# A hybrid decoder trunk on one core: start-up transfers put in line, the first statistics moved into the third weight tile, attention scores of four heads issued together, and the squares before the pool mixer summed on VectorE

## What is computed

```python
def rmsnorm(x, g):
    return x * rsqrt(mean(x * x, -1) + EPS) * g
def swiglu(h, w_gate, w_up, w_down):
    return (silu(h @ w_gate) * (h @ w_up)) @ w_down
for i in range(2):
    x = x + 0.5 * swiglu(rmsnorm(x, g[i, 0]), ...)
    h = rmsnorm(x, g[i, 1])
    x = x + (moba_attention(h, w_qkv, w_o) if i == 0 else pool_mixer(h, pool_w, pool_scale))
    x = x + 0.5 * swiglu(rmsnorm(x, g[i, 2]), ...)
return rmsnorm(x, final_gain)
```

## Time and profile before

| | |
|---|---|
| median of 3 executions | 890.85 us (889.71 to 890.87) |
| profiled execution, its time | 889.62 us |
| its span, first to last instruction | 887.7 us |
| TensorE busy | 874.7 us (99%) |
| VectorE, ScalarE busy | 630.9 us (71%), 468.8 us (53%) |
| mean granted TensorE clock | 0.995 of full speed |

### The profile page before, as it was taken

How to read it: one execution, slowest core, us unless ns; L and a number is a source line. 1 busy time by engine, 2 the same in 40 slices (tenths; PEclk the granted TensorE clock), 3 DMA queues, 4 the chain that set the end, 5 groups by cost and what they waited for, 6 DMA issues and landing times.

```text
span 887.7 us, 12466 instructions
## 1 busy us (share of the span) xinstructions
PE 874.7 (99%) x5252; PEld 768.7 (87%) x5252; DVE 630.9 (71%) x718; ACT 468.8 (53%) x557; POOL 34.1 (4%) x49
## 2 busy tenths in 40 slices
PE   7999999999999999999999999999999999999997
PEld 6888888889998988888888888888889988888885
DVE  5997776668777598777667697776666698777452
ACT  5765554445555566555544475555544675555441
POOL 1580000000000000000000000000000000000000
PEclk9999999999999999999999999999999999999999
DMA  7786656555544438665565566565566177565431
GB/s 247 228 244 196 190 178 197 181 190 175 159 142 143 143 97 256 188 190 190 168 205 181 176 204 193 188 190 188 177 200 191 49 217 222 188 218 187 154 119 47
DMA packets 154167, 159.69 MB, mean 180 GB/s; under 512 B 2888, under 2 KB 152448, under 8 KB 154112
## 3 DMA queue, kind: packets, MB, share of 16 engines
q1 hardware_dynamic: 152672, 157.30, 55.8%
q10 hardware_dynamic: 1440, 1.60, 0.5%
HBM read 157.84 MB, written 1.05 MB: 179 GB/s over the span
## 4 chain that ended last, share of the span: by engine, by line
PE 97%; DVE 1%; ACT 0%; issue 0%; POOL 0%; DVEq 0%; POOLq 0%
PE psum L413 95%; PE psum L694 1%; PE psum L680 1%; PE psum L587 0%; DVE w_lo L1151 0%; DVE x L1157 0%; PE psum L580 0%; DVE soft L979 0%; PE psum L453 0%; ACT xg L777 0%; DVE w_lo L1143 0%; ACT scratch L848 0%; DVE band L1080 0%; DVE h_all L1232 0%; DVE scratch L1083 0%
## 5 line engine op out<-in xcount | busy, mean ns | idle before, releaser
L413 PE MATMUL psum<-xg,w_hi 128*128 128x512 f32 (+1 forms) x1664 | 491.4, 380 | 2.9 <-DVE w_lo L1143 2.9
L960 DVE TENSOR_TENSOR w_lo<-raw,w_hi 128x2048 fp32r<-128x2048 f32 (+1 forms) x150 | 336.3, 2243 | 119.8 <-ACT w_hi L768 119.8
L413 PEld LDWEIGHTS psum<-xg,w_lo 128*128 128x128 f32 x1536 | 289.6, 189 | 62.7
L768 ACT ACTIVATE w_hi<-raw 128x2048 fp32r<-128x2048 f32 (+1 forms) x150 | 279.5, 1865 | 92.0 <-PE psum L413 92.0
L413 PE MATMUL psum<-xg,w_lo 128*128 128x256 f32 x1536 | 313.3, 279 | 0.0
L413 PEld LDWEIGHTS psum<-xg,w_hi 128*128 128x128 f32 x1664 | 254.8, 189 | 5.8 <-issue 4.7
L413 PE MATMUL psum<-h_all,w_hi 128*128 128x512 f32 (+1 forms) x656 | 189.4, 374 | 0.7 <-DVE h_all L1232 0.7
L413 PEld LDWEIGHTS psum<-h_all,w_lo 128*128 128x128 f32 x592 | 111.4, 188 | 23.4
L413 PE MATMUL psum<-h_all,w_lo 128*128 128x256 f32 x592 | 121.8, 278 | 0.0
L413 PEld LDWEIGHTS psum<-h_all,w_hi 128*128 128x128 f32 x656 | 100.3, 189 | 1.5 <-issue 1.5
L803 ACT ACTIVATE scratch<-psum 128x512 f32<-128x512 f32 x44 | 26.2, 595 | 86.0 <-PE psum L413 86.0
(11 more groups left out here) (108 smaller groups left out, 489.8 us busy)
## 6 DMA issues: line engine op xcount, KB each, us to landing
raw<-in_ffn_w_up_dram SPq DMA_DIRECT2D x43, 1024.0 KB, 5.3
raw<-in_ffn_w_gate_dram SPq DMA_DIRECT2D x42, 1024.0 KB, 5.3
raw<-in_ffn_w_down_dram SPq DMA_DIRECT2D x24, 1024.0 KB, 5.1
raw<-in_attn_w_qkv_dram SPq DMA_DIRECT2D x12, 1024.0 KB, 5.1
raw<-in_ffn_w_down_dram SPq DMA_DIRECT2D x20, 512.0 KB, 4.3
raw<-in_ffn_w_down_dram SPq DMA_DIRECT2D x12, 768.0 KB, 4.3
raw<-in_attn_w_o_dram SPq DMA_DIRECT2D x4, 1024.0 KB, 5.0
band<-in_x_dram SPq DMA_DIRECT2D x4, 256.0 KB, 5.4
```

The lines of the kernel that those rows point to most:

```text
L413: return nc.tensor.matmul(out, stationary, moving, start=start, stop=stop, skip_group_check=True)
L768: nc.scalar.activation(w_hi[:, n % SPL, 0:size], raw[:, n % RAW, 0:size], ACT.Copy).then_inc(hi_split, 1)
L960: nc.vector.tensor_tensor(w_lo[:, n % SPL, 0:size], raw[:, n % RAW, 0:size], w_hi[:, n % SPL, 0:size].bitcast(f32), ALU.subtract).then_inc ...
```

## The change

In the head, SyncE waits until the second piece of tile 0 has landed before it issues tiles 1 and 2. TensorE does 8 + 3 + 5 idle transposes around the gains and the first two pieces of x in place of 12 ahead of them, and transposes pieces 2 and 3 of x ahead of k = 0 and k = 2 (ahead of k = 2 and k = 4 before). The first statistics move behind the first half of tile 2 (gate of group 1), tile 3 follows, and VectorE splits tile 3 before it takes the mean.

In the first three quads of attention all four heads' scores are issued together, then the q and k products, then the four heads' transposes, the v product, and the four heads' values; `prob` and `probT` get four buffers. ScalarE does all four heads' exponentials before it rounds weights, VectorE all four heads' softmax before it splits them.

At the pool boundary the squares are summed on VectorE (the last two chunks one by one), and TensorE needs two products with ones, in the middle of the last pool product. Half of `pool_u` is scaled by VectorE. The up tile of the last FFN is no longer split in the FFN before, but by halves inside `mixer_boundary`. ScalarE loads the root's table at the start of `down`. FFNs 1 to 3 start when their gate tile is split, not gate and up tile both.

```diff
+            sp.wait_ge(piece_loaded[1], 16)
             ffn(0, 0, 0)
...
-                            if norm == 0 and k % 2 == 0 and 0 < k < DC - 2:
-                                x_transposes(k // 2 + 1)
+                            if norm == 0 and k % 2 == 0 and k < DC - 4:
+                                x_transposes(k // 2 + 2)
...
                 if f == 0:
                     column_chunks(0, 0, range(DC))
                     column_chunks(0, 1, range(DC))
+                    pe.wait_ge(x_done, DC // 2)
+                    column_chunks(1, 0, range(DC // 2))
+                    pe.wait_ge(x_done, DC)
                     statistics(norm)
...
-                else:
-                    weights(n0 + 1)
+                    column_chunks(1, 0, range(DC // 2, DC))
+                    weights(n0 + 3)
+                    pe.wait_ge(newton, 1)
+                    column_chunks(1, 1, range(DC))
+                else:
+                    weights(n0)
...
-            for _ in range(12):
-                nc.tensor.transpose(psum[:, 2, 0:P], ident[:, :], ident[:, :])
-            x_transposes(0)
+            idle_transposes(8)
...
+            x_transposes(0)
+            idle_transposes(3)
             x_transposes(1)
+            idle_transposes(5)
...
                 scores(j, 0)
-                between(0)
-                transposes(j, 0)
-                scores(j, 1)
-                between(1)
-                values(j, 0)
-                transposes(j, 1)
                 if j < QUADS - 1:
+                    scores(j, 1)
+                    between(0)
+                    between(1)
+                    transposes(j, 0)
+                    transposes(j, 1)
                     between(2)
+                    values(j, 0)
                     values(j, 1)
...
+                        if g == NPG - 1 and t == 0 and m == 1:
+                            statistics(4)
...
-                if g == 1:
-                    for c in range(DB):
-                        token_squares(4, c)
...
+            def load_root():
+                nc.scalar.activation(table[:, 1:2], table[:, 0:1], ACT.Sqrt)
+
             def down(f):
+                load_root()
...
-                for t in range(TT):
-                    last = nc.scalar.activation(pool_u[:, g, t, :], psum[:, g, t * GW:(t + 1) * GW], ACT.Copy,
-                                                scale=rstd_p[:, t:t + 1])
-                last.then_inc(pool_u_scaled, 1)
+                nc.scalar.activation(pool_u[:, g, 0, :], pool_acc(g, 0), ACT.Copy,
+                                     scale=rstd_p[:, 0:1]).then_inc(pool_u_scaled[0], 1)
...
+                nc.vector.tensor_scalar(pool_u[:, g, 1, :], pool_acc(g, 1), rstd_p[:, 1:2], None,
+                                        ALU.mult).then_inc(pool_u_scaled[1], 1)
...
-            def mixer_boundary(norm, scalar, per_chunk=False):
+            def split_lo_ahead(n, half):
+                dve.wait_ge(hi_split, n + 1)
+                part = slice(half * ROWS // 2, (half + 1) * ROWS // 2)
+                nc.vector.tensor_tensor(w_lo[:, n % SPL, part], raw[:, n % RAW, part], w_hi[:, n % SPL, part].bitcast(f32),
+                                        ALU.subtract).then_inc(lo_split if half else up_half, 1)
+
+            def mixer_boundary(norm, scalar, per_chunk=False, split_ahead=None):
                 for c in range(DB + 1):
+                    if split_ahead is not None and c == DB - 1:
+                        rest_chunk(norm, 2 * c - 2)
+                        rest_chunk(norm, 2 * c - 1)
+                        split_lo_ahead(split_ahead, 0)
...
             split_lo_half(2, 1)
+            split_lo(3)
             dve.wait_ge(late_T, 1)
...
-            split_lo(3)
             refine_rstd(0)
```

More of the change, by code:

```diff
@@ L442, in statistics @@
                 pe.wait_ge(sq_sum_done, FOLDS.index(norm) + 1)
-                last = mm(psum[:, b, 0:SEQ], ones[:, :], sq_sum[:, :], start=True, stop=True)
-                for t in range(TT if norm == 1 else 0):
+                if norm != 4:
+                    last = mm(psum[:, b, 0:SEQ], ones[:, :], sq_sum[:, :], start=True, stop=True)
+                for t in range(TT if norm in (1, 4) else 0):
                     last = mm(psum[:, b, SEQ + t:SEQ + t + 1], sq_sum[:, t * P:(t + 1) * P], ones[:, 0:1],
@@ L549, in ffn @@
                     column_chunks(0, 1, range(EARLY, DC))
-                for j in range(1, GROUPS):
+                for j in range(1 if f else 2, GROUPS):
                     gate_up(j)
@@ L584, in _, with idle_transposes @@
             pe.wait_ge(consts_built, 2)
-            for _ in range(12):
-                nc.tensor.transpose(psum[:, 2, 0:P], ident[:, :], ident[:, :])
-            x_transposes(0)
+            def idle_transposes(count):
+                for _ in range(count):
+                    nc.tensor.transpose(psum[:, 2, 0:P], ident[:, :], ident[:, :])
+            idle_transposes(8)
             pe.wait_ge(gains_loaded, 16)
@@ L913, in _ @@
             for j in range(QUADS):
-                for half in range(2):
-                    heads = (2 * half, 2 * half + 1)
-                    for hh in heads:
+                if j < QUADS - 1:
+                    for hh in range(QH):
                         exps(QH * j + hh)
-                    split_hi(ATT0 + 3 * j + 2 + half + SPL)
-                    for hh in heads:
+                    split_hi(ATT0 + 3 * j + 2 + SPL)
+                    split_hi(ATT0 + 3 * j + 3 + SPL)
+                    for hh in range(QH):
                         copy_probT(j, hh)
+                else:
+                    for half in range(2):
+                        heads = (2 * half, 2 * half + 1)
+                        for hh in heads:
+                            exps(QH * j + hh)
+                        split_hi(ATT0 + 3 * j + 2 + half + SPL)
+                        for hh in heads:
+                            copy_probT(j, hh)
                 split_hi(ATT0 + 3 * j + 4 + SPL)
@@ L1057, in down @@
                         add_squares(norm, pair - 1)
-                    split_lo(n + 1 + SPL)
+                    if f == 2 and pair == DB - 1:
+                        dve.wait_ge(sq_added, FOLDS.index(4) * (DB - 1) + DB - 2)
+                        nc.vector.tensor_tensor(sq_sum[:, :], sq[:, 0, :], sq[:, 1, :], ALU.add).then_inc(sq_added, 1)
+                    else:
+                        split_lo(n + 1 + SPL)
                     for d in (2 * pair, 2 * pair + 1):
@@ L1216, in _ @@
             for j in range(QUADS):
-                for half in range(2):
-                    heads = (2 * half, 2 * half + 1)
-                    for hh in heads:
+                if j < QUADS - 1:
+                    bias_and_max(j, 0)
+                    for hh in range(1, QH):
                         bias_and_max(j, hh)
-                    for hh in heads:
-                        normalise(QH * j + hh)
-                    if j == 0 and half == 0:
+                        normalise(QH * j + hh - 1)
+                    normalise(QH * j + QH - 1)
+                    if j == 0:
                         qkv_scale(0, 2)
-                    split_lo(ATT0 + 3 * j + 2 + half + SPL)
-                    if j < QUADS - 1:
-                        qkv_scale(j + 1, half)
+                    for s in range(2):
+                        split_lo(ATT0 + 3 * j + 2 + s + SPL)
+                        qkv_scale(j + 1, s)
+                else:
+                    for half in range(2):
+                        heads = (2 * half, 2 * half + 1)
+                        for hh in heads:
+                            bias_and_max(j, hh)
+                        for hh in heads:
+                            normalise(QH * j + hh)
+                        split_lo(ATT0 + 3 * j + 2 + half + SPL)
                 split_lo(ATT0 + 3 * j + 4 + SPL)
```

98 lines of the change are left out of this document (65 added, 33 removed).

## The result

The changed kernel takes 881.7 us (median of 4 executions, 881.35 to 882.02), the kernel before, on the same chip, 890.86 us (4 executions, 889.71 to 891.12). The ratio is 0.9903 with a 95% interval of 0.9891 to 0.9915: 9.2 us less. 881.2 was forecast. The profiled executions went from 889.62 to 881.35 us, 8.3 us less; the new one has a span of 879.3 us, and its mean granted clock is 0.999.

What follows compares the result with a forecast made beforehand. TensorE, busy 99% of the span, bounds the kernel. Head 4.0, attention 1.5 and pool boundary 3.5 sum to 9.0 us, taking the profiled 889.62 to 880.6 and the median to 881.2; range 878.5 to 884.5 us.

Steps and rivals of the forecast that it cites:

- The head: Start of the kernel: TensorE's start on tile 4 moves from 36.5 to 32.5 us, 4.0 us; bounds 2.3 and 4.9.
- TensorE waits 1.0 us for tile 4: Head: TensorE there at 31.7 us, VectorE's split of tile 4 done at 32.5, so a new wait of 0.8 us.
- VectorE's chain to have only one change: Head: same operations in another order, except that VectorE now waits 0.5 us for ScalarE's root.
- The rival: Head gives little, chance 0.14: late first x piece, clock fall or late halves of tile 1; 2.0 us gained, 883.2.
- Attention: First three quads: six merged blocks of scores and values save 0.25 us each, 1.5 us; bounds nothing and 3.0.
- the regroupings are neutral: Attention rival, chance 0.08: the 0.2 us is a pipeline's end, not the switch; merged blocks cost the same, 882.7.
- fall of the clock: Attention rival, chance 0.03: half-array values and scores in succession lower the clock; 6 us falls cost 9.0 us, giving 891.7.
- The pool boundary: Before the last FFN: 3.9 us less at its start, 0.4 lost behind, 3.5 us; bounds 2.0 and 4.2.
- The new wait: Pool boundary: TensorE waits for the scaled pieces behind the statistics, +0.7 us.
- The 0.4 us: Last FFN: waits from VectorE's half splits and what queues behind them, last x pair, last rests and sums, +0.4 us.
- The 1.5 us of clock: Pool boundary: the 24 matmuls behind the products with ones run at full clock, -1.5 us.
- The median: Whole kernel: the new median may lie 0 to 1.2 us over the new profile of 880.6; predicted 881.2.

Runs made afterwards that it cites:

- hold_first_fill: The changed kernel with SyncE waiting for the first gate piece in place of the second, and 8 idle transposes in place of 5: 880.97 us.
- scores_apart: The changed kernel with the second pair's scores put back behind the q product in the first three quads: 882.64 us.
- trans_apart: The changed kernel with the first pair's transposes put between the q and the k product; scores and values stay merged: 881.39 us.
- narrow_extra: The changed kernel with 14 unused products with one column of ones (28 rows) behind the second pool product: 886.08 us, a fourth execution of 3063.89 left out.
- wide_extra: The changed kernel with 30 unused idle transposes, 128 columns wide, behind the second pool product: 884.54 us.
- head_only: The kernel before with only the head's part of the change: 885.28 us, ratio 0.9952.
- attn_only: The kernel before with only attention's part of the change: 889.29 us over 12 executions, ratio 0.9984.
- pool_only: The kernel before with the pool boundary's part, the up tile's halves, the root's table and the gate-tile start of FFNs 1 to 3: 886.6 us.

## Why the prediction was right

The bottleneck was read rightly: time came from TensorE alone, and only in the three stretches named. The sum was 9.0 us, made of 4.0, 1.5 and 3.5; the profiled pair gives 3.25, 2.1 and 3.2, which is 8.55 of stage gains against 8.3 us between the two times. All three sizes were off: the head by -0.75, attention by +0.6, the boundary by -0.3. That the head's miss and attention's nearly cancel is luck.

- **The head**, 4.0 forecast, 3.25 measured. Its mechanism holds: VectorE's last piece moved by 3.55 us (forecast 3.7), the root is exposed for 0.48 us (0.5), the clock stays up, and without the idle transposes it does not. TensorE waits 1.0 us for tile 4 (0.8), but the two agree only since both engines are late: TensorE is there at 32.4 us in place of 31.7, and tile 4 can start at 33.4 in place of 32.5. The mis-sized term is the one that took VectorE's chain to have only one change: the held-back halves of tile 1 are late and cost 0.63 us. The rival named this, halves there at 10.9 to 12.3 us where VectorE wants them at 12.4; the first came at 12.2, but ScalarE's rounding of 1.06 us lies between landing and VectorE. hold_first_fill takes that wait away, and tile 4 moves by 0.4 us. The other 0.1 us is what smaller terms leave, such as the last piece, 0.15 us later than forecast.
- **Attention**, 1.5 forecast, 2.1 measured. Scores count and transposes don't, as forecast (scores_apart, trans_apart); for values only the rest of the 0.7 us speaks. The price for a merged block was 0.25 us from two rows and is 0.35 (0.7 us a quad, two blocks) or 0.38 (scores_apart). That the regroupings are neutral is out; no fall of the clock was seen behind values and scores (granted clock 1.00 from 200 to 300 us).
- **The pool boundary**, 3.9 forecast and 3.6 measured at the start of the last FFN, then 0.4 lost: 3.2. The new wait was taken at 0.7 us and costs 1.0 from start to start (0.8 in the list of waits). The 0.4 us are the size that was forecast, but the last rests and the sums, to which they were put down among others, come in time: it is two weight splits that TensorE waits for. The 1.5 us of clock in it are real for the pair of profiles, and narrow_extra against wide_extra gives 1.4. But they are not due in every execution: head_only's profile had none to lose, attn_only's lost 3 us. What the structure alone saves is 12.87 - 10.78 = 2.1 us.
- **The median**. The new profile was the fastest of its four, as was the old, so the median lies 0.35 us over it; it was taken 0.6 over, which takes back 0.25 of the 0.75 us by which the profile itself was missed.

What stays open: whether an ordinary execution is faster without the hold, what decides whether the clock falls behind the 32 narrow rows, and how the head's gain divides among the parts that weren't taken apart.

## What to carry to other kernels

Where TensorE waits for first transfers, give it cheap full-width transposes instead of idling: eight of them were worth 1.0 us here. Queue only as much behind the first needed pieces as leaves them on time, and count the engines between landing and use when a transfer is held back. Sum squares on an engine with room rather than by one-column products, and put all work on part of the array in one block. Value a part of a change by its own stage in the trace: in these profiles what the clock did elsewhere added 1.5 us to the head's 3.25 and took 2.6 us from attention's 2.1.

## What the runs showed that I had not expected

The same 32 one-column rows were followed by full clock (head_only) and by 1.2 GHz for some 3 us (before); in attn_only the clock was down for 6 to 7 us from within the rows on. The code at that place is the same. The changed kernel, without these rows, spreads by 0.7 us (881.35 to 882.02), attn_only by 4.6; but the rows aren't the only thing that makes executions differ, since pool_only has none either and spreads by 1.4.

The record of the clock can miss a fall. In attn_only's window at 10 to 12 us above it says 1.00, with 9 matmuls in 2.0 us, as many as in the window of before at 0.50; in the changed kernel there are 13. This is TensorE's timeline in that window:

```profile
9.80 1.05 PE L414 MATMUL psum<-xg,w_hi 128*128 128x512 f32 x2
10.65 0.63 PE L414 MATMUL psum<-xg,w_lo 128*128 128x256 f32 x2
```

A pair of 512 wide matmuls takes 1.05 us in place of 0.63 to 0.70, as a pair does at 9.26 us in the kernel before, where the record has the clock down. The Trainium skill, TensorE: Matmul & The Clock Gate, section Seeing it yourself, warns that the clock's trace events are unreliable on trn2; this case agrees. The spacing of matmuls is the surer sign.
